# A fused decoder trunk on one core: the first stage's modulation by single feature tiles instead of pairs

## The reference, cut to what matters

```python
c_act = jax.nn.silu(c)                                # (1, 1024)
mod = c_act @ ada_w[l] + ada_b[l]                     # (1, 6*1024)
sh_m, sc_m, g_m, sh_f, sc_f, g_f = jnp.split(mod, 6, axis=-1)
h = rms_norm(x, norm_mix_g[l]) * (1 + sc_m) + sh_m
u = h @ w_in                                          # (512, 3*1024)
```

## Time and profile before

| | before |
|---|---|
| median of 3 runs | 1168.9 us (1168.03 to 1169.14) |
| profiled execution's own time | 1168.89 us |
| its span | 1167.1 us |
| mean granted clock of TensorE | 0.997 |
| TensorE busy | 1148.8 us (98%) |
| DVE busy | 872.4 us (75%) |
| ACT busy | 546.9 us (47%) |

### The profile page before, as it was taken

The page is one execution under the profiler, slowest core; times in us unless marked ns, Lnnn a source line. Parts: engine busy times, 40 slices in busy tenths (PEclk is TensorE's granted clock), DMA queues, the critical chain, the costliest instruction groups (busy, mean ns, idle before and its releaser), DMA issues.

```text
span 1167.1 us, 16194 instructions
## 1 busy us (share of the span) xinstructions
PE 1148.8 (98%) x5751; PEld 965.8 (83%) x5751; DVE 872.4 (75%) x1188; ACT 546.9 (47%) x874; POOL 25.2 (2%) x37
## 2 busy tenths in 40 slices
PE   6999999999999999999999999999999999999998
PEld 4788888988888888888978888888988888888887
DVE  5656888886675675545889889897987778769794
ACT  5422333641241241233678778774675444545521
POOL 2000000000000000200020000000000000000000
PEclk8999999999999999999999999999999999999999
DMA  9767566376666656333245455464034323332311
GB/s 334 246 183 250 181 197 198 109 216 198 201 180 197 205 174 200 105 91 90 71 129 139 120 133 135 110 163 145 24 104 126 95 87 108 108 114 85 109 55 72
DMA packets 200987, 168.87 MB, mean 145 GB/s; under 512 B 5620, under 2 KB 173724, under 8 KB 200924
## 3 DMA queue, kind: packets, MB, share of 16 engines
q1 hardware_dynamic: 200732, 167.92, 48.4%
q10 hardware_dynamic: 160, 0.06, 0.0%
q0 software_dynamic: 32, 0.07, 0.0%
HBM read 153.24 MB, written 2.10 MB: 133 GB/s over the span
## 4 chain that ended last, share of the span: by engine, by line
PE 89%; DVE 6%; ACT 2%; issue 1%; DMA 1%; SPq 1%; DVEq 0%; ACTq 0%
PE bank L734 23%; PE bank L736 23%; PE bank L735 23%; PE bank L989 4%; PE bank L991 4%; PE bank L990 4%; PE bank L1159 1%; PE bank L1141 1%; PE bank L1131 1%; PE bank L1132 1%; DVE w_lo L1832 1%; DMA first_raw<-in_sc_w_in 1%; SPq L448 0%; PE bank L866 0%; DVE x L1916 0%
## 5 line engine op out<-in xcount | busy, mean ns | idle before, releaser
L734 PE MATMUL bank<-h_hi,w_hi 128*128 128x512 f32 (+1 forms) x864 | 325.0, 376 | 1.6 <-DVE w_lo L1832 1.6
L736 PE MATMUL bank<-h_hi,w_lo 128*128 128x512 f32 (+1 forms) x864 | 322.7, 374 | 0.0
L735 PE MATMUL bank<-h_lo,w_hi 128*128 128x512 f32 (+1 forms) x864 | 322.7, 373 | 0.0
L1298 ACT ACTIVATE w_hi<-raw 128x1024 fp32r<-128x1024 f32 x151 | 158.5, 1054 | 152.4 <-DMA raw<-in_mlp_w 115.4
L1832 DVE TENSOR_TENSOR w_lo<-raw,w_hi 128x1024 fp32r<-128x1024 f32 x151 | 183.7, 1220 | 40.4 <-ACT w_hi L1298 39.6
L734 PEld LDWEIGHTS bank<-h_hi,w_hi 128*128 128x128 f32 x864 | 162.7, 188 | 30.1 <-issue 2.0
L736 PEld LDWEIGHTS bank<-h_hi,w_lo 128*128 128x128 f32 x864 | 162.7, 188 | 29.0
L735 PEld LDWEIGHTS bank<-h_lo,w_hi 128*128 128x128 f32 x864 | 162.8, 188 | 28.2 <-issue 0.2
L734 PE MATMUL bank<-g_hi,w_hi 128*128 128x512 f32 (+1 forms) x416 | 154.9, 372 | 0.0
L736 PE MATMUL bank<-g_hi,w_lo 128*128 128x512 f32 (+1 forms) x416 | 153.5, 369 | 0.0
L735 PE MATMUL bank<-g_lo,w_hi 128*128 128x512 f32 (+1 forms) x416 | 153.4, 369 | 0.0
(11 more groups left out here) (271 smaller groups left out, 1689.6 us busy)
## 6 DMA issues: line engine op xcount, KB each, us to landing
raw<-in_mlp_w SPq DMA_DIRECT2D x96, 512.0 KB, 4.0
ada_raw<-in_ada_w SPq DMA_DIRECT2D x40, 1024.0 KB, 5.5
w_raw<-in_mlp_w SPq DMA_DIRECT2D x32, 512.0 KB, 3.4
raw<-in_sc_w_in SPq DMA_DIRECT2D x20, 512.0 KB, 4.1
ada_first<-in_ada_w SPq DMA_DIRECT2D x32, 256.0 KB, 7.8
raw<-in_w_kv SPq DMA_DIRECT2D x16, 512.0 KB, 3.9
raw<-in_q_w SPq DMA_DIRECT2D x8, 512.0 KB, 4.8
keys<-qk SPq DMA_DIRECT2D x16, 256.0 KB, 3.1
```

Of the source, the lines that this page charges most:

```text
L734: mm(out[:, cols], weights_hi, hi[:, k, cols], start=(k == 0), stop=False)
L735: mm(out[:, cols], weights_hi, lo[:, k, cols], start=False, stop=False)
L736: return mm(out[:, cols], weights_lo, hi[:, k, cols], start=False, stop=(k == KT - 1))
L1298: go(w_hi[:, jj, :, :], raw[:, jj, :, :], ACT.Copy).then_inc(hi_ok, 1)
```

## The change

Quarters of two tiles become eight units of one feature tile each (shift and scale, 256 columns). `ada_first` gets four slots of half the size. A unit comes in four transfers of 256 KB (input tiles 0 to 3 and 4 to 7, shift and scale apart, pieces of 512 B instead of 1 KB). The group's weights come by single input tiles (256 KB), with semaphores of their own for even tiles. Unit 0 is not shared with DVE: TensorE multiplies its 16 blocks of 128 x 128 with columns of c (`first_unit_sums`). Units 1 to 7 go as the quarters did, with half the columns. All tiles are scaled and shifted by ACT (`first_tile`); `odd_tile` is gone. The rows of x are scaled in two pieces, the first 256 columns ahead. x tiles 0 and 1 are copied out earlier, x tiles 5 to 7 a step later each, and x tile 7 now stands ahead of `split(1, 0)`. Lines that are removed with the old functions are left out here; the functions are shown above.

```diff
 GROUP = 4
-QUARTERS = 4
+UNITS = KT
+ADA_SLOTS = 4
...
-    ada_first, = stacked(region_g, [("ada_first", [P, 2, KT, 2, D // QUARTERS], F32)])
+    ada_first, = stacked(region_g, [("ada_first", [P, ADA_SLOTS, KT, 2, P], F32)])
...
         wf_loaded = sem("wf_loaded")
-        ada_in = [[sem(f"ada_in{s}{k}") for k in range(KT)] for s in range(2)]
+        ada_in = [[sem(f"ada_in{s}{half}") for half in range(2)] for s in range(ADA_SLOTS)]
+        first_in = [sem(f"first_in{q}") for q in range(KT // 2)]
+        first_hi_ok = sem("first_hi_ok")
+        first_lo_ok = sem("first_lo_ok")
         ada_more = [sem("ada_more0"), sem("ada_more1")]
...
@@ -437,21 +441,26 @@
             for t in range(TT):
                 sp.dma_start(x_rows[:, t, :], x_in[0, t * P:(t + 1) * P, :]).then_inc(x_loaded[t], 16)
+            ada_rows = ada_w[0].rearrange("(k p) n -> p k n", p=P)
+            def ada_unit(e):
+                for half in range(2):
+                    if e == ADA_SLOTS:
+                        sp.wait_ge(ada_turned, 1)
+                    elif e > ADA_SLOTS:
+                        sp.wait_ge(*((ada_strip if half else ada_stepped), (e - ADA_SLOTS) * STRIPS))
+                    k = slice(half * STRIPS, (half + 1) * STRIPS)
+                    for n in range(2):
+                        c0 = n * D + e * P
+                        sp.dma_start(ada_first[:, e % ADA_SLOTS, k, n, :], ada_rows[:, k, c0:c0 + P]
+                                     ).then_inc(ada_in[e % ADA_SLOTS][half], 16)
+            first_w = sc_w_in[0].rearrange("(k p) n -> p k n", p=P)
+            for k in range(KT):
+                ada_unit(k)
+                sp.dma_start(first_raw[:, k, :], first_w[:, k, D:D + GROUP * P]).then_inc(
+                    raw_in[k // 2] if k % 2 else first_in[k // 2], 16)
             sp.wait_ge(first_used, 1)
             load_block(0, c_g(GROUP))
...
@@ -843,34 +852,42 @@
+            def unit(j):
+                if j >= 2:
+                    pe.wait_ge(tile_ok, j - 1)
+                for t in range(TT):
+                    if j == 0:
+                        pe.wait_ge(*((unit_ok, t + 1) if t < 2 else (unit_rest_ok, t - 1)))
+                    if j == 2:
+                        pe.wait_ge(*((unit_ok, 3 + t) if t < 3 else (unit_rest_ok, 3)))
+                    v = turn(bank[4 + j % 2][:, t * P:(t + 1) * P], x_unit[:, t, j * P:(j + 1) * P], ident[:])
+                v.then_inc(unit_turned, 1)
+            def first_unit_sums(half):
+                pe.wait_ge(ada_in[0][half], 32)
+                for k in range(half * STRIPS, (half + 1) * STRIPS):
+                    for n in range(2):
+                        one = mm(bank[6][:, n:n + 1], ada_first[:, 0, k, n, :], c_act[:, k:k + 1], start=(k == n == 0),
+                                 stop=(k == KT - 1), skip_group_check=True)
+                if half:
+                    one.then_inc(ada_turned, 1)
+            def unit_strips(e):
+                pe.wait_ge(ada_red, e)
+                pe.wait_ge(ada_in[e % ADA_SLOTS][1], 32 * (e // ADA_SLOTS + 1))
                 for i in range(STRIPS):
                     k = STRIPS + i
+                    mm(bank[6][32 * i:32 * i + 32, 0:2 * P], c_wide[:, k, :], ada_first[:, e % ADA_SLOTS, k, :, :],
+                       start=True, stop=True, skip_group_check=True).then_inc(ada_strip, 1)
+            def unit_sum(e):
+                pe.wait_ge(ada_added, e)
+                for n in range(2):
+                    c = n * KT + e
                     one = mm(bank[6][:, n:n + 1], ada_acc[:, c * P:(c + 1) * P], ones[:, 0:1], start=(n == 0),
                              stop=True, skip_group_check=True)
                 one.then_inc(ada_turned, 1)
...
             def first_products(k, blocks=range(GROUP)):
-                pe.wait_ge(lo_ok, k // 2 + 1)
+                pe.wait_ge(lo_ok if k % 2 else first_lo_ok, k // 2 + 1)
                 pe.wait_ge(h_ok, H_MIX0 + k + 1)
                 for b in blocks:
...
@@ -904,34 +921,23 @@
             pe.wait_ge(cols_ok, 2)
             for j in range(4):
                 x_turn(j)
+            pe.wait_ge(c_ok, 1)
+            first_unit_sums(0)
+            unit(0)
+            first_unit_sums(1)
+            unit(1)
+            x_turn(4)
             pe.wait_ge(c_ok, 2)
+            for k in range(KT - 1):
+                unit_strips(k + 1)
+                first_products(k, range(0, 2))
+                unit_sum(k + 1)
+                first_products(k, range(2, GROUP))
+                if k < KT - 2:
+                    unit(k + 2)
+                if k >= GROUP:
+                    x_turn(k + 1)
+            first_products(KT - 1)
...
@@ -1386,6 +1392,15 @@
+            def x_tile(j):
+                act.wait_ge(x_turned, j + 1)
+                go(x[:, j, :], bank[X_BANK[j]][:], ACT.Copy).then_inc(x_ok, 1)
+            def scaled_rows(t, cols):
+                go(x_unit[:, t, cols], x_rows[:, t, cols], ACT.Copy, scale=tok[:, 3, t:t + 1]).then_inc(unit_rest_ok, 1)
...
             go(tok[:, 1, :], tok[:, 1, :], ACT.Exp, scale=-0.5).then_inc(norm_y, 1)
+            for j in range(2):
+                x_tile(j)
             act.wait_ge(inv_ok, 1)
             for t in range(2, TT):
+                scaled_rows(t, slice(0, FIRST_COLS))
+            x_tile(2)
+            def split_first(k):
+                act.wait_ge(raw_in[k // 2] if k % 2 else first_in[k // 2], 16)
+                go(first_hi[:, k, :], first_raw[:, k, :], ACT.Copy).then_inc(hi_ok if k % 2 else first_hi_ok, 1)
+            def first_tile(j):
                 act.wait_ge(unit_turned, j + 1)
+                act.wait_ge(mod_ok, j + 1)
                 if j >= 4:
                     act.wait_ge(h_ok, H_MIX0 + j - 3)
+                go(hs_slot(j, ALL), bank[4 + j % 2][:], ACT.Identity, bias=mcol(0, 0, j),
+                   scale=gains[:, 0, j:j + 1]).then_inc(tile_ok, 1)
+                act.wait_ge(tile_ok, j + 1)
                 go(h_hi[:, j, :], hs_slot(j, ALL), ACT.Copy).then_inc(hh_ok, 1)
             split_first(0)
+            first_tile(0)
+            x_tile(3)
+            scaled_rows(TT - 1, slice(FIRST_COLS, D))
             x_tile(4)
+            for k in range(1, KT):
+                split_first(k)
+                first_tile(k)
+                if k > GROUP:
+                    x_tile(k)
             split(1, 0)
+            act.wait_ge(unit_rest_ok, 3)
+            act.wait_ge(unit_ok, 5)
             split(1, 1)
...
@@ -1980,49 +1986,43 @@
+            def unit_acc(e):
+                return ada_acc[:, 0:2 * D].rearrange("p (a e c) -> p a e c", a=2, e=UNITS)[:, :, e, :]
+            def unit_steps(e, first=0, last=STRIPS):
+                acc = unit_acc(e)
+                dve.wait_ge(ada_in[e % ADA_SLOTS][0], 32 * (e // ADA_SLOTS + 1))
                 for k in range(first, last):
+                    row = ada_first[:, e % ADA_SLOTS, k, :, :]
                     if k == 0:
                         one = ts(acc, row, c_act[:, 0:1], None, ALU.mult)
                     else:
+                        dve.wait_ge(ada_stepped, (e - 1) * STRIPS + k)
                         one = stt(out=acc, in0=row, scalar=c_act[:, k:k + 1], in1=acc, op0=ALU.mult, op1=ALU.add)
                     one.then_inc(ada_stepped, 1)
+            def unit_add(e):
+                acc = unit_acc(e)
+                dve.wait_ge(ada_stepped, e * STRIPS)
+                dve.wait_ge(ada_strip, e * STRIPS)
+                tt(acc, bank[6][:, 0:2 * P].rearrange("p (a c) -> p a c", a=2), acc, ALU.add).then_inc(ada_added, 1)
+            def split_first(k):
+                dve.wait_ge(hi_ok if k % 2 else first_hi_ok, k // 2 + 1)
+                tt(first_lo[:, k, :], first_raw[:, k, :], first_hi[:, k, :],
+                   ALU.subtract).then_inc(lo_ok if k % 2 else first_lo_ok, 1)
+            def unit_gain(e):
+                both = lambda t: t[:, 0:2 * KT].rearrange("p (a b) -> p a b", a=2)[:, :, e:e + 1]
+                dve.wait_ge(ada_turned, e + 1)
+                tt(both(mod), bank[6][:, 0:2].rearrange("p (a b) -> p a b", a=2), both(ada_bias),
                    ALU.add).then_inc(ada_red, 1)
+                dve.wait_ge(ada_red, e + 1)
+                gain(0, 0, 1, R_MIX, e + 1, (e, e + 1))
             def first_low(j):
                 h_low(H_MIX0 + j, j, None, h_hi, h_lo)
...
@@ -2050,42 +2050,29 @@
+            def scaled_rows(t, cols):
+                ts(x_unit[:, t, cols], x_rows[:, t, cols], tok[:, 3, t:t + 1], None, ALU.mult).then_inc(unit_ok, 1)
             for t in range(2):
+                scaled_rows(t, slice(0, FIRST_COLS))
+            for t in range(2):
+                scaled_rows(t, slice(FIRST_COLS, D))
+            unit_gain(0)
             split_first(0)
+            scaled_rows(2, slice(FIRST_COLS, D))
+            unit_steps(1, 0, 2)
             first_low(0)
+            unit_steps(1, 2)
+            for k in range(1, KT):
+                unit_add(k)
```

(40 more changed lines are left out.)

124 lines of the change are left out of this document (6 added, 118 removed).

## The result

| | before | changed |
|---|---|---|
| median of 11 runs | 1168.03 us | 1171.93 us |
| lowest to highest | 1167.32 to 1169.14 | 1170.21 to 1174.52 |
| profiled execution: own time, span | 1168.89, 1167.1 us | 1171.70, 1169.9 us |

The ratio is 1.0037, with a 95% interval of 1.0029 to 1.0045: slower by 0.37%, and more than the 0.2% that this measurement can tell. A second set of five runs gave 1.0034 (1.0021 to 1.0047).

What follows compares the result with a forecast made beforehand. TensorE was taken as the bound, without a gap from 24.07 us to the next group at 55.07 us. A later next group (+1.1) and half clock (+1.3) made +2.4 us on 1168.89: 1171.3 us, range 1167.8 to 1173.8.

Steps and rivals of the forecast that it cites:

- The sum: Whole kernel: +1.1 us at the stage's end and +1.3 us of half clock, +2.4 us on 1168.89: 1171.3 us.
- The start: Opening: first sum's result at 15.95 us, DVE's 3.1 us after it, first products at 19.15 us instead of 24.07.
- The round: Loop from sum to sum through ACT, DVE and six products: 4.81 us per tile, 4.89 with an x tile.
- The clock: Opening: granted clock falls in TensorE's idle time before the first products, back after three microseconds of products: +1.3 us.
- The tail: Stage's end: next group waits for ACT's z copy, starts 3.1 us after products(7), at 56.2 us, 1.1 us later.
- The transfers: Pieces of 512 B at 326 GB/s: 4.0 us per unit with weights, mattering only over 5.1 us; costed at nothing.
- A: Rounds: TensorE alone sets the pace, 4.25 us per tile; next group 3.3 us earlier, 1165.6 us; chance 0.10.
- B: Opening: the clock stays up, or is back before the first products: 1170.0 us; chance 0.25.
- C: First round: the low clock lasts over all of it: 1172.4 and up to 1173.3 us; chance 0.15.
- D: Rounds: the clock swings since TensorE waits in each; two rounds at half clock, +7.5 us, 1176.4 us; chance 0.05.
- E: Unit transfers: pieces of 512 B fall under 240 GB/s and steps wait: +2.8 us, 1174.1 us; chance 0.05.
- F: Opening: the edit brings nothing because the start is not earlier; not likely, counted with B.

Runs made afterwards that it cites:

- third: Changed kernel with the next tile's sum behind nine products of the running tile instead of six: 1177.80 us, ratio 1.0079.
- loop2_tail: Changed kernel, next sum ahead of all products, strips of unit k+2 between their halves, x tile 7 after split(1, 0), block 1 before the modulation: 1172.71 us, ratio 1.0039.
- shared: Changed kernel with unit 0 shared between DVE and TensorE again, in place of TensorE's 32 one-column passes: 1170.76 us, ratio 1.0027.
- shared_tail: Changed kernel with unit 0 shared with DVE, x tile 7 after split(1, 0), and block 1 before the first 1 MB of modulation: 1169.13 us, ratio 1.0010.
- before_fill: Kernel before the change with seven idle products on TensorE between the first sum and the second pair of transposes: 1167.50 us, ratio 0.9994.

## Why the prediction was right, point by point

**The sum.** Forecast +2.4 us on the profiled execution, measured +2.8; 1171.3 us against a median of 1171.9. The forecast case is the one that came true, with its direction. But that the two medians differ by 3.9 us, 1.5 more than forecast, and the forecast is still only 0.6 us off, is luck: it was added to 1168.89 us, a long execution of the kernel before, 0.9 us above the median of 1168.03. Of the 1.5 us that is 0.9; 0.4 is the opening, and 0.2 is the profiled execution's place below its own median.

**The start: right, 0.6 us late.** The result of the first sum came at 16.65 us instead of 15.95 and the products at 19.78 instead of 19.15, for three reasons: the four tiles of x ended at 12.38 us instead of 12.18, the first eight sums and the unit cost 0.17 us more, and the second half of the sums, which ran partly at half clock, 0.3 us more. (15.95 + 3.1 is 19.05, so the working has 0.1 us to spare.) DVE's 3.1 us from that result to the first products were right to 0.1 us, and a multiply-add of 256 columns took 0.48 to 0.49 us, as the slope had it.

**The round: right.** 4.81 us forecast, 4.77 measured (27.45 to 32.21 us between two sums on the chain); with an x tile 4.89 forecast, about 4.85 measured. That it is a loop through six products is shown by third (+0.69 us per round for three products) and by loop2_tail (4.42 us once it is opened). The waits of 0.3 us stand where they were forecast. In the last round TensorE waited 0.87 us; I had counted a unit there that no longer exists.

**The clock: right in size, wrong in place.** The first round cost 1.27 us more than the others, for 1.3 forecast. But the clock did not fall in an idle time at 18.6 us; it fell at 15.7 us, in the one-column sums, and was back at 22.5 us. The step that failed is "TensorE ends its strips at about 17.4 us and idles until 19.15, as long as now, so I expect the granted clock to fall again": it took idle time for the only thing ahead of a fall, and no row of before shows TensorE for long on such sums. At half clock the strips ended at 19.46 us, and the idle time was 0.3 us. No row stands behind the three microseconds of low clock either. That the six products lay in the low stretch all the same is luck: it began 2.9 us earlier than forecast and lasted 6.8 us.

The changed kernel has long executions of about 1174 us (four of eleven). They do not explain the 1.5 us: the other seven have a median of 1171.5 us, 0.4 below that of all. The long execution of third spends 3.4 us on each half of the sums, since full clock came at 25.1 us only. That the long runs of the changed kernel itself are of this kind is argued from third's profile, not shown. The record speaks for it in part. Of its sixteen executions in two sets five took over 1174 us; the mean granted clock of three of them reads 1.000, as third's does, which has no fall on record, and none of the eleven shorter ones reads that. The other two read 0.999 and 0.995.

**The tail: right on its releaser, wrong on the reason.** ACT's z copy released the next group, 3.37 us after products(7) for 3.1 forecast. But ACT waited 1.07 us for block 1. The step "so it is hidden" looked only at who waits for the 1 MB of modulation, not at the weight block behind it in SP's queue, which had to wait until the 1 MB could go out: 4.8 us.

**The transfers: wrong in rate, right in effect.** 291 GB/s, where I took 326 from the nearest row. A unit with its weights took 4.3 us (8.58 to 25.88 us is four of SP's issues of a unit) instead of 4.0, below the 5.1 us from which it would have mattered in the rounds. In shared, where the start is earlier, the strips of unit 1 do wait 1.05 us for their transfer.

**The rivals.** A did not come: the loop was closed. B was not seen in the changed kernel, but shared_tail behaves like it. C did not come: the low clock ended inside the first round, and the long executions lie above its 1173.3 us. The one that was profiled (third) lost its 3.5 us ahead of the products, with only four of them at half clock, a case that no rival had. D did not come: four waits of 0.3 us in rounds of 4.77 us left the granted clock at 1.00. The rule of the Trainium skill that the prediction set beside it (TensorE: Matmul & The Clock Gate, "A second HAM failure mode: psum-queue depth-cycling") is not borne out by this trace for waits of this size. E did not come, nor did F: the start was 4.3 us earlier.

## What to carry to other kernels

Cutting a pipelined step in half brings the first result earlier, but it doubles how often the chain sum, gain, tile, split is passed through. Write down the loop from one result to the next through all engines and compare it with the bound engine's own work per step, before and after the cut. And read the queue behind the stage too: a wait that is 0.3 us today becomes 1.8 us as soon as the stage in front of it is faster.

## What the runs showed of the hardware

- The granted clock fell to half while TensorE was busy without a gap, on 32-bit products with a single column (eight of them, 16 records, in 1.9 us), and not only in idle time: at 15.7 us in the changed kernel's profile, at 15.1 to 15.2 us in its three repeats. In the kernel before it fell 0.7 us into an idle time of 1.8 us.
- The profile's granted clock can read 1.00 while instructions run at half speed: in third's profile it is 1.00 from 12 to 25 us, with single products of 512 columns 0.43 us apart until 25.1 us; in before_fill's the transposes stand 0.21 us apart until 17.6 us, where 0.11 is full speed. The distance between equal instructions is the safer reading.
- When full speed first came differed from one execution to the next, with the same work on TensorE up to there: at 12.3 us in the changed kernel, at 25.1 us in third. It moved the start of the products by 3.5 us.
- Transfers of the modulation in pieces of 512 B ran at 291 GB/s, in pieces of 1 KB at 348 GB/s, with the queues full in both cases. A weight block, also in pieces of 512 B, ran at 326 GB/s, so the size of the pieces alone does not set the rate.
- With seven idle products in a wait of 1.8 us no fall of the clock is on record in any of eleven executions (mean granted clock 1.000 in each). It was worth 1.6 us in the profile and 0.8 us by the medians, not told apart from nothing; DVE's steps then set the pace.
